# Turning diff outputs and probabilities outside TensorE in a hybrid attention layer

## The reference

```python
h = rms_norm(x, norm1_g)
proj = h @ w_in                       # (256, 6152): q, k, v of 8 fox heads and 8 diff heads, forget logits
# 8 forgetting-attention ("fox") heads of width 128, causal, with a bias from cumulated forget gates
p_f = softmax(where(causal, q_f @ k_f.T * 128**-0.5 + cq - ck, -1e30));  o_f = p_f @ v_f
# 8 differential ("diff") heads: two 64-wide halves of q and k, partial rotary, chunk mask of 64
p_d = softmax(where(chunk, q_d @ k_d.T * 64**-0.5, -1e30))               # for each half c
a_d = p_d[c=0] - lam * p_d[c=1]
o_d = rms_norm(a_d @ v_d, diff_subln_g) * (1 - lambda_init)
x = x + concat(o_f, o_d) @ w_out
u = causal depthwise conv(rms_norm(x, norm2_g) @ w_up);  gate, val = split(u)
out = x + (silu(gate) * val) @ w_down                                    # d_ff 5504
```

## Time and profile before

| | us |
|---|---|
| median of 3 runs (1044.97 to 1047.63) | 1047.46 |
| the profiled execution, its own time | 1047.41 |
| its span, first to last instruction | 1045.6 |
| PE busy with matmuls | 1039.4 (99%) |
| ACT busy | 785.5 (75%) |
| DVE busy | 745.7 (71%) |
| POOL busy | 20.5 (2%) |
| DMA traffic | 217.77 MB, 208 GB/s over the span |

### The profile page before, as it was taken

One profiled execution on the slowest core, in us unless ns is written; L12 is line 12 of the kernel. 1 busy time (PEld: TensorE's weight loads), 2 busy tenths in 40 slices (PEclk: granted clock), 3 DMA queues, 4 the chain that ended last, 5 costly groups with the idle time before them and its releaser, 6 DMA issues.

```text
span 1045.6 us, 16399 instructions
## 1 busy us (share of the span) xinstructions
PE 1039.4 (99%) x5330; PEld 941.8 (90%) x5330; DVE 745.7 (71%) x1238; ACT 785.5 (75%) x1376; POOL 20.5 (2%) x27
## 2 busy tenths in 40 slices
PE   9999999999999999999999999999999999999998
PEld 8999999999988888888888888888889988888887
DVE  6888878778767666576776776876867678866664
ACT  7777666788858884879788788798797778755553
POOL 0101010000000000000000000000000000000000
PEclk9999999999999999999999999999999999999999
DMA  9756676676766666666565575665756766666664
GB/s 355 234 160 189 193 235 201 215 245 225 237 213 198 203 199 203 202 218 201 184 221 198 187 222 194 201 216 185 219 184 187 235 204 202 203 202 206 205 206 144
DMA packets 75438, 217.77 MB, mean 208 GB/s; under 512 B 15850, under 2 KB 18418, under 8 KB 75250
## 3 DMA queue, kind: packets, MB, share of 16 engines
q1 hardware_dynamic: 75376, 216.99, 65.3%
HBM read 212.69 MB, written 4.27 MB: 207 GB/s over the span
## 4 chain that ended last, share of the span: by engine, by line
PE 83%; DVE 6%; DMA 4%; ACT 4%; issue 2%; SPq 1%; DVEq 0%; ACTq 0%
PE ps L605 14%; PE ps L604 14%; PE ps L606 14%; PE ps L635 7%; PE ps L633 7%; PE ps L634 7%; PE ps L397 3%; PE ps L399 3%; PE ps L398 3%; DMA raw<-in_win 3%; PE ps L582 2%; PE ps L581 2%; PE ps L580 2%; DVE w_lo L1117 2%; ACT w_hi L681 1%
## 5 line engine op out<-in xcount | busy, mean ns | idle before, releaser
L1117 DVE TENSOR_TENSOR w_lo<-raw,w_hi 128x1024 fp32r<-128x1024 f32 (+1 forms) x406 | 463.4, 1147 | 245.1 <-ACT w_hi L681 241.7
L681 ACT ACTIVATE w_hi<-raw 128x1024 fp32r<-128x1024 f32 (+1 forms) x406 | 398.1, 987 | 167.3 <-PE ps L635 74.8
L604 PE MATMUL ps<-w_hi,xs 128*128 128x512 f32 (+1 forms) x704 | 263.4, 374 | 0.0
L605 PE MATMUL ps<-w_lo,xs 128*128 128x512 f32 (+1 forms) x704 | 263.4, 374 | 0.0
L606 PE MATMUL ps<-w_hi,xs 128*128 128x512 f32 (+1 forms) x704 | 263.4, 374 | 0.0
L397 PE MATMUL ps<-w_hi,xs 128*128 128x384 f32 (+1 forms) x512 | 170.9, 334 | 0.6 <-DVE w_lo L1399 0.6
L398 PE MATMUL ps<-w_lo,xs 128*128 128x384 f32 (+1 forms) x512 | 167.0, 326 | 0.0
L399 PE MATMUL ps<-w_hi,xs 128*128 128x384 f32 (+1 forms) x512 | 167.0, 326 | 0.0
L606 PEld LDWEIGHTS ps<-w_hi,xs 128*128 128x128 f32 x704 | 133.1, 189 | 17.2
L605 PEld LDWEIGHTS ps<-w_lo,xs 128*128 128x128 f32 x704 | 133.1, 189 | 17.2
L604 PEld LDWEIGHTS ps<-w_hi,xs 128*128 128x128 f32 x704 | 133.1, 189 | 17.2
(11 more groups left out here) (162 smaller groups left out, 922.1 us busy)
## 6 DMA issues: line engine op xcount, KB each, us to landing
raw<-in_wrest SPq DMA_DIRECT2D x278, 512.0 KB, 4.1
raw<-in_win SPq DMA_DIRECT2D x117, 384.0 KB, 3.8
raw<-in_wrest SPq DMA_DIRECT2D x16, 384.0 KB, 3.0
p_scratch<-pdT SPq DMA_DIRECT2D x11, 192.0 KB, 2.4
p_read<-p_scratch SPq DMA_DIRECT2D x44, 48.0 KB, 2.9
xtok<-in_xtok SPq DMA_DIRECT2D x4, 512.0 KB, 13.0
xv<-in_xtok SPq DMA_DIRECT2D x4, 512.0 KB, 6.3
raw_ahead<-in_w SPq DMA_DIRECT2D x5, 392.0 KB, 8.4
```

The costliest lines, as they stand in the source:

```text
L604: pe.matmul(o, xh, wh, start=(k == 0), stop=False, skip_group_check=True)
L605: pe.matmul(o, xh, wl, start=False, stop=False, skip_group_check=True)
L681: act.activation(slot(w_hi, s, w), slot(raw, s, w), ACT.Copy).then_inc(hi_ready, 1)
L1117: dve.tensor_tensor(slot(w_lo, s, w), slot(raw, s, w), f32(slot(w_hi, s, w)), ALU.subtract).then_inc(split_done, 1)
```

## The change

Five edits, in four functions of PE's program and what belongs to them on the other engines:

1. **Outputs of diff heads.** `out_transposes` is gone. DVE transposes the normed output in 32x32 blocks (`turn_o`, from `on` to `onT`, 128x256), SP stores `onT` to a second DRAM scratch and reads it back in four DMAs (`store_o`, `read_o`); ACT and DVE split it from there two frames after its scores (`mix_hi`, `mix_lo` at b=5 of frame f+2; head 1 at b=1 of frame 4). `mix_lo` of a diff head is two instructions now.
2. **Probabilities.** `P0` goes from 4 to 2 and `P_STOP` from 15 to 16: heads 2, 3 and 15 take the way by DRAM as well. Head 2 is stored after SP's step (2, 7), read at (3, 1), copied by ACT in step (3, 3) and used by PE after piece b=5 of frame 3 (before: b=4). Head 15 is used from `p_read` by `block_values` after the fifth piece of the output projection.
3. **Values later.** `copy_p` moves from b=0 to b=1, `values` and the squares from b=2 to b=4, the statistics to b=5, the guess, the norm and `turn_o` to b=6.
4. **The first four pieces** are used in another order (`high_parts_first`): high x high as soon as the high parts are there, then low x high, then the product with the weights' low parts.
5. `WARM_UP` goes from 11 to 7.

The core of the diff:

```diff
-WARM_UP = 11
+WARM_UP = 7
...
-P0, P_STOP = 4, HEADS - 1
+P0, P_STOP = 2, HEADS
 BLOCK_AT = dict(scores=5)
 MOVES = {1: (0, 5), 2: (5, 16)}
 DIFF_AT = dict(turn=2, scores=3)
-TRAIL_AT = dict(values=2, sums=2, norm=2, turn=4, hi=5, lo=6)
+TRAIL_AT = dict(copy=1, values=4, sums=4, stats=5, guess=6, norm=6, mix=5)
 CONV_TAIL = {11 + 3 * t: (FULL - 1, t, BATCH) for t in range(BATCH)} | {28 + 3 * t: (FULL, t, LAST) for t in range(LAST)}
 FORGET_AT = dict(scale=0, logits=0, exp=1, log=2, turn=3)
...
+        def by_blocks(t, h):
+
+            return t.rearrange("p (k h i t) -> p h k i t", k=2, h=2, i=4)[:, h]
+
+        def landed_o():
+            return o_read[:].rearrange("p (i m t) -> p m i t", i=4, m=M)
 
...
+            def store_o(f):
+                sp.wait_ge(o_turned, f)
+                if f > 1:
+                    sp.wait_ge(o_landed, 64 * (f - 1))
+                sp.dma_start(o_d, onT[:]).then_inc(o_stored, 16)
+
+            def read_o(f):
+                sp.wait_ge(o_stored, 16 * f)
+                if f > 1:
+                    sp.wait_ge(mixlo_done, f - 1)
+                for j in range(4):
+                    src = o_d[:, j * 64:(j + 1) * 64].rearrange("(i r) c -> r i c", i=4)
+                    sp.dma_start(o_read[32 * j:32 * (j + 1), :].rearrange("r (i c) -> r i c", i=4), src).then_inc(o_landed, 16)
...
+                    if f == 2 and b == 7:
+                        store_p(2)
+                    if f == 3:
+                        if b == 1:
+                            read_p(2)
+                        if b == 3:
+                            store_o(1)
+                        if b == 4:
+                            store_p(3)
+                        if b == 5:
+                            read_o(1)
+                        if b == 6:
+                            read_p(3)
+                    if 4 <= f <= H + 2 and b == 0:
+                        store_o(f - 2)
+                    if 4 <= f <= H + 2 and b == 2:
+                        read_o(f - 2)
+                    if 4 <= f <= H + 1 and b == 3:
                         store_p(f)
-                    if f <= H + 1 and b == 5:
+                    if 4 <= f <= H + 1 and b == 5:
                         read_p(f)
...
-                if not first:
-                    pe.wait_ge(mixlo_done, f - 1)
+                if kind == "diff" and not first:
+                    pe.wait_ge(onorm_done, f - 1)
...
-            def out_transposes(f):
-
-                pe.wait_ge(onorm_done, f)
-                for m in range(M):
-                    last = pe.transpose(bank(B_O, S + m * P, P), on[:, m * P:(m + 1) * P], ident)
-                last.then_inc(oturn_done, 1)
...
-                    if trail and b == TRAIL_AT["turn"]:
-                        out_transposes(f - 1)
...
+            def high_parts_first(h, b, g, k2):
+
+                W, kt = QKV if h else QKV + H, 2 * b + k2
+                wh, wl = weave(slot(w_hi, g, W, k2 * W)), weave(slot(w_lo, g, W, k2 * W))
+                xh, xl = [[xs[:, kt * 2 * S + i * S + m * P:kt * 2 * S + i * S + (m + 1) * P] for m in range(M)] for i in range(2)]
+                pe.wait_ge(hi_ready if k2 else hi_first, g + 1)
+                pe.wait_ge(xhi_ready, kt + 1)
+                for m in range(M):
+                    pe.matmul(bank(2 * h + m, 0, W), xh[m], wh, start=(kt == 0), stop=False, skip_group_check=True)
+                pe.wait_ge(xs_ready, kt + 1)
+                for m in range(M):
+                    pe.matmul(bank(2 * h + m, 0, W), xl[m], wh, start=False, stop=False, skip_group_check=True)
+                pe.wait_ge(split_done if k2 else lo_first, g + 1)
+                for m in range(M):
+                    last = pe.matmul(bank(2 * h + m, 0, W), xh[m], wl, start=False, stop=False, skip_group_check=True)
+                return last
+
...
+                    if g < HALVED:
+                        last = high_parts_first(h, b, g, k2)
+                        continue
...
-                if b == 0:
-                    prob_transposes(2, "diff")
                 if b == 3:
-                    out_transposes(1)
-                    pe.wait_ge(pT_ready, 2)
                     transposes(3, 0, "diff")
                 if b == 4:
+                    scores(3, "diff")
+                if b == 5:
                     values(2, 1, "diff")
-                    scores(3, "diff")
-                if b == 6:
-                    out_transposes(2)
-                if b == 7:
-                    prob_transposes(3, "diff")
             for f in range(4, H + 1):
...
-                if b == 0:
-                    prob_transposes(HEADS - 1, "fox")
-                if b == 1:
-                    values(HEADS - 1, 0, "fox")
                 attention_steps(HEADS, 1, "fox", b, OUT_AT)
+                if b == LAST_BLOCK_VALUES:
+                    block_values(HEADS - 1, 0)
...
+            def copy_p(f, unscaled=False):
...
+                to = pT[:].rearrange("p (s i t) -> p s i t", i=4, s=3)
+                landed = p_read[:].rearrange("p (i s t) -> p s i t", i=4, s=3)
+                if unscaled:
+
+                    act.activation(to[:, 0:2], landed[:, 0:2], ACT.Copy, scale=r1[:, 0:1])
+                    act.activation(to[:, 2], landed[:, 2], ACT.Copy, scale=r1[:, 1:2]).then_inc(p_copied, 1)
+                    return
+                act.activation(to, landed, ACT.Copy).then_inc(p_copied, 1)
...
+                act.wait_ge(o_landed, 64 * f)
+                act.activation(by_blocks(mxt, 0), landed_o(), ACT.Copy, scale=sg[:]).then_inc(mixhi_done, 1)
...
+                if b == TRAIL_AT["copy"]:
+                    copy_p(f - 1)
...
+                    if isinstance(f, int) and f == 4 and b == 1:
+                        mix_hi(1, "diff")
+                    if isinstance(f, int) and f <= H + 2 and b == TRAIL_AT["mix"]:
+                        mix_hi(f - 2, "diff")
...
+            def turn_o(f):
+
+                dve.wait_ge(onorm_done, f)
+                if f > 1:
+                    dve.wait_ge(o_stored, 16 * (f - 1))
+                dve.transpose(onT[:].rearrange("p (j m t) -> p j m t", j=4, m=M),
+                              on[:].rearrange("p (m j t) -> p j m t", j=4, m=M)).then_inc(o_turned, 1)
+
...
+                    for m in range(M):
+                        last = dve.scalar_tensor_tensor(out=by_blocks(mxt, 1)[:, m], in0=landed_o()[:, m], scalar=sg[:],
+                                                        in1=by_blocks(f32(mxt), 0)[:, m], op0=ALU.mult, op1=ALU.subtract)
+                    last.then_inc(mixlo_done, 1)
```

101 lines of the change are left out of this document (46 added, 55 removed).

## The result

| kernel | median, us | ratio to the kernel before, 95% interval |
|---|---|---|
| before | 1047.05 (6 runs) | 1 |
| changed | 1055.44 (6 runs, 1053.38 to 1057.13) | 1.0084 [1.0073, 1.0095] |

The change makes the kernel slower by 8.4 us. The forecast was 1053.0, in a range of 1044.5 to 1057.0. The profiled execution took 1056.23 us (span 1054.4), 8.8 more than the one of before. In the changed kernel's lines, the turn of q and k is L451, the scores L460, values L487, the splits L724 and L1164, and the rotary part L1734 and L1737.

What follows compares the result with a forecast made beforehand. PE, busy 99% of the span, bounds the kernel, so only its matmuls and waits count. From 1047.41 us, gains of 5.25 and losses of 10.8 give 1053.0, range 1044.5 to 1057.0.

Steps and rivals of the forecast that it cites:

- The two waits of values: PE's waits for ACT's copy of the probabilities in frames 6 and 8 go: 1.6 us gained.
- The start: First pieces, high parts first with seven warm-ups: PE starts earlier, 0.6 us gained (0.45 to 0.75).
- The 0.3 us for head 15: Of PE's 0.7 us wait for head 15's copy, about 0.3 goes; the next turn waits soon after.
- Turns of heads 5 to 7: PE waits for POOL's rotary part, 1.2 us each (0.65 to 1.7), 3.6 in all.
- DVE's order: Output's norm and transpose stand ahead of the sum of squares on DVE; some 0.6 us remains (0 to 1.05).
- the chain of 6.43: Head 5, from the projection's last matmul to POOL's rotary end: 6.43 us, covered before by six value matmuls.
- The third rival: POOL's rotary part meets no two-input DVE work; five chains shorten 1.24 us each, 1043.2 to 1046.9; chance 0.16.
- Head 2's values: Frame 3: PE waits for the read-back by DRAM and ACT's copy, 2.1 us lost (1.0 to 3.0).
- Head 4's turn: ACT free late in frame 3 and DVE's added work delay the rotary part: 2.5 us lost (0.3 to 3.2).
- the fourth rival: Stores and reads on SP ahead of weight loads delay ACT's splits, eight heads 4 us more: 1057; chance 0.16.
- Head 8: Turn: uncovered chain 1.05, late read-back of head 5's output, norm's 0.6: 2.3 us lost (1.05 to 3.6).
- The fox heads: Two heads after head 8: new DVE work ahead of a split, mostly hidden, 0.3 us lost (0 to 0.6).

Runs made afterwards that it cites:

- four edits: Changed kernel with rotary part on DVE, head 2's values after b=6, head 15's read-back behind the load, frame 10's splits at b=6: 1047.29 us, 1.0012.
- six edits: The kernel of four edits, plus copy of probabilities at b=2 and forget gates' exponential, logarithm, turn at b=2, 3, 4: 1045.71 us, 1.0002.

## Why the prediction was right, and where it was not

**What bounds.** Right: an edit counted only through what PE waits for. DVE and ACT kept their shares.

**Gains.** The two waits of values came as priced, and the 25 transposes are gone. The start, 0.6 forecast, measured 0.5 alone by the ratio (1.6 less to 0.6 more), which holds both 0.6 and nothing; in the changed profile 1.0 us was gained up to the turn of head 1 and 0.4 lost right behind it. The 0.3 us for head 15 was wrong in sign: its 1.0 us of PE work, moved away, had covered head 16's turn, and its read-back on SP held up a load of weights. That is the same uncovering that I priced for heads 4 to 8 and did not look for at the end.

**Turns of heads 5 to 7.** 3.6 forecast, 3.7 measured. The mechanism was the forecast's, and so was its split: 0.65 for the chain that lost its cover and 0.55 for DVE's order, 0.59 measured. What I did not see is how the two hang together: with DVE's order undone only 0.10 was left, since POOL's second instruction then took 0.46 in place of 1.05 us, and the chain of 6.43 became 5.84, as short as three pieces. The row at 94.77 that the prediction calls head 5's last matmul is the first one of the next piece (the last starts at 94.61); the 6.43 and the 5.85 are both counted from it, so their difference stands.

**POOL beside DVE.** The third rival put this at 1.24 us a head and gave it 0.16. It was not what the changed kernel did: its rows are 1.38 and 1.05 as before. But the mechanism exists. With the norm moved, the second instruction took 0.46, and the small DVE instruction waited in its place. The Trainium skill, page "SBUF — State Buffer", section "Who interferes with whom", has the first to start hold the port; the trace agrees, with 0.69 us for an instruction of 128x2 that ended when POOL's did.

**Heads 2 and 4.** Head 2's values: 2.1 forecast, 1.4 measured. On a clock that was 1.0 us ahead of the forecast's, the read-back landed at 70.96 (72.3 forecast, so 0.3 earlier) and PE came at 70.4 (71.1, so 0.3 later). Head 4's turn: 2.5 forecast and measured. The prediction's working has a slip there: 73.2, a split and the exponentials give 75.8 and not 75.5, and from 75.5 its terms add up to 80.4 and not 80.9. In the changed kernel's rows, counted like the 6.43 above (from 76.51), ACT's squares start at 77.41, 0.70 later than for head 5, and DVE's sum at 79.41, 2.00 after them in place of 0.87: 0.58 + 0.70 + 1.13 = 2.4 us, and 0.07 for the semaphore. Of the 1.13 some 0.59 is DVE's order, as at the other turns; the rest, about 1.2 us with the 0.70, came with ACT's idle time, by this estimate. The 0.7 us of head 4's scores, which waited for ACT's copy, was no term of mine.

**Head 8.** 2.3 forecast, 1.3 measured. The read-back behind the late piece was 0.7 us late for ACT (152.36), but the squares, 0.5 late in my sum, were not: they started 0.20 behind the frame's first matmul (154.49 to 154.69), as before. DVE's sum started 1.55 after the squares where it was 1.28, so its order cost 0.3 and not 0.6.

**The fox heads.** 0.3 forecast, 3.2 measured. This is the step that failed: "For the two fox heads that follow, the new DVE work (1.07 us) stands ahead of a split and most of it falls into the lead of the splits over PE". I priced DVE's work there and not SP's queue, in which a load of x of 512 KB stands just ahead of head 8's read-back. ACT waited 3.0 us for it. That is the fourth rival's mechanism, not spread over eight heads at 0.5 but in one place.

**The sum.** That the time lies inside the range is in part luck. Head 2's values and head 8 were taken 1.7 us too large; the fox heads, heads 15 and 16, the split behind head 1's turn and head 4's scores together 5.3 too small. Had only the second kind occurred, the time would have been 1058, outside the range.

**The granted clock.** I expected no fall near the start and none fell that cost anything to speak of; I did not look at head 4's turn. Of the changed kernel's six runs three have a mean clock of 0.998 and three of 1.0. They overlap in time (1054.8 to 1057.1, and 1053.4 to 1056.2). If the fall is the one seen in the profile of the kernel without the outputs' DMAs, it costs each of the three about 1.4 us, a part of the price that no step of mine had.

## What to carry to other kernels

Small work that stands in front of a wait may be cover: before it is moved, read how long the chain behind that wait is from end to end, at every place of the kind. One chain can hold up more than one thing: here the same norm stood ahead of the turn and of the split of the next piece, so a later turn only moved the wait. The stores and read-backs of the outputs cost nothing at most of their places, and 3 us by place at the one where a load of 512 KB stood ahead of them; list the queue at each of their places. A wait that is gone from a profile is not yet time gained: single repairs took 1 to 7 us of waits away at their places, and the time moved by anything from 4.7 us up to 1.9 down, where four together gave 7.5.

## What the runs showed of the hardware

- After PE had waited 2.4 us at head 4's turn, its matmuls ran at half speed for nine matmuls in three profiles (norm behind the next norm, head 8's output later, no DMAs of outputs: granted clock 0.83 over 10 us) and at full speed in three others with the same wait (changed kernel, x loads later, head 15's read-back later: 1.00). In the three kernels without that wait (head 2 later, four edits, six edits) all 28 runs have a mean clock of 1.0.
- A DVE instruction of 128x2 took 0.69 us where it began beside a POOL instruction, against 0.15 for the same one alone, and POOL's 1.05 us became 0.46 when no weight split ran beside it.
- The same DMA of 384 KB at the start landed 1.1 us apart in two executions with the same issues ahead of it, and the split that waits for it starts at 6.56 to 7.67 in thirteen profiles.
- The last DMA of head 8's read-back took 5.2 us from issue to landing where a load of 512 KB had been issued ahead of it, and 2.0 us where it had not.
